# The expert stage of a PEER layer on one core: transposed weights from the host, sums kept in PSUM, unrolled rings

## What is computed

```
eidx, g = the 16 best experts of each head and their softmax   # P x 8 x 16
u   = expert_u[eidx]                       # (P, 8, 16, D)
act = gelu(einsum("phkd,pd->phk", u, x))
out = einsum("phk,phkd->pd", g * act, expert_v[eidx])
```

## Time and profile before

| | us |
|---|---|
| median of 3 runs | 4127.46 (4125.85 to 4132.15) |
| span of the profiled execution | 4126.5 |
| phases ahead of the expert stage | to about 1877 |
| expert stage | 1877 to 4051 |
| final phase | 4051 to 4126.5 |

### The profile page before, as it was taken

One profiled execution on the slowest core, in us unless ns is written; L12 is line 12 of the kernel. 1 busy time (PEld: TensorE's weight loads), 2 busy tenths in 40 slices (PEclk: granted clock), 3 DMA queues, 4 the chain that ended last, 5 costly groups with the idle time before them and its releaser, 6 DMA issues. The chain is left out here.

```text
span 4126.5 us, 52192 instructions
## 1 busy us (share of the span) xinstructions
PE 3607.3 (87%) x16733; PEld 2479.9 (60%) x16733; DVE 2800.2 (68%) x5843; ACT 798.0 (19%) x1845; POOL 1709.6 (41%) x1654
## 2 busy tenths in 40 slices
PE   8679899995857777846999999999999999999992
PEld 1435454442347777844667766777676776667771
DVE  1523233334938777898787877788777887778876
ACT  0101111012105787601111111111111111111110
POOL 0000000001105998705565655555555655555540
PEclk9689999997989999978999999999999999999996
DMA  7233433302241334407999999999989999999973
GB/s 253 80 57 37 36 47 51 34 6 103 82 144 43 90 86 103 115 2 260 351 328 337 349 322 348 328 351 327 337 322 351 333 336 343 327 354 326 350 271 112
DMA packets 453585, 870.03 MB, mean 211 GB/s; under 512 B 194637, under 2 KB 244045, under 8 KB 453206
## 3 DMA queue, kind: packets, MB, share of 16 engines
q0 software_dynamic: 153008, 555.83, 37.3%
q1 hardware_dynamic: 300344, 311.30, 26.0%
HBM read 805.98 MB, written 61.06 MB: 210 GB/s over the span
## 5 line engine op out<-in xcount | busy, mean ns | idle before, releaser
L1460 PE MATMUL v<-vb,w 128*128 128x512 f32 x2640 | 1159.2, 594 | 4.9 <-DVE acc L1547 4.9
L1444 POOL DMA_INDIRECT ring<-in_expert_u,eu x512 | 616.7, 1204 | 603.7 <-DVE dots L1532 300.2
L1460 PEld LDWEIGHTS v<-vb,w 128*128 128x128 f32 x2640 | 493.5, 191 | 577.9 <-issue 571.2
L1444 POOL DMA_INDIRECT ring<-in_expert_v,ev x512 | 612.0, 1195 | 441.0 <-DVE acc L1542 282.8
L1490 PE MATMUL a<-h2T_hi,uT 128*128 128x320 f32 x4096 | 713.8, 321 | 0.0
L1490 PEld LDWEIGHTS a<-h2T_hi,uT 128*128 128x128 f32 x4096 | 621.7, 188 | 61.2 <-issue 61.2
L1542 DVE SCALAR_TENSOR_TENSOR acc<-ring,wgt,acc 128x1024 f32 x508 | 650.7, 1281 | 10.3
L1532 DVE CUSTOM_DVE_ANT_1 ring<-ring,h2T 128x1024 f32<-128x1024 f32 x512 | 602.4, 1218 | 0.6 <-DMA ring<-in_expert_u,eu 0.6
L652 PE MATMUL z<-W,hT 128*128 128x512 f32 x1152 | 507.9, 594 | 23.3 <-DMA bh<-in_b_in 23.3
L1245 POOL TENSOR_SCALAR hotJ<-cst,pickT 128x128 f32<-128x128 f32 x560 | 424.9, 778 | 124.4 <-ACT pickT L1232 119.9
L1514 ACT ACTIVATE ga<-a 128x320 f32<-128x320 f32 x256 | 112.1, 438 | 1802.0 <-PE a L1490 1456.1
(11 more groups left out here) (266 smaller groups left out, 3216.0 us busy)
## 6 DMA issues: line engine op xcount, KB each, us to landing
ub<-in_expert_u SPq DMA_DIRECT2D x128, 512.0 KB
vb<-in_expert_v SPq DMA_DIRECT2D x32, 2048.0 KB
weight_d<-stage SPq DMA_DIRECT2D x10, 4096.0 KB, 20.9
wt<-weight_d SPq DMA_DIRECT2D x128, 320.0 KB, 5.3
wa<-in_w_ada SPq DMA_DIRECT2D x12, 2048.0 KB, 8.0
W<-in_w_in SPq DMA_DIRECT2D x32, 512.0 KB, 10.0
wq<-in_w_pq SPq DMA_DIRECT2D x4, 2048.0 KB, 17.0
ring<-in_expert_u,eu POOLq DMA_INDIRECT x512
```

The lines of the kernel that those rows point to most:

```text
L1444: pool.indirect_dma_start(ring[:, r, :], None, table, bass.IndirectOffsetOnAxis(idx[:, k % SLOTS:k % SLOTS + 1], 0)).then_inc(landed[r], 16)
L1460: mm = pe.matmul(vps[(NU * (s // GS) + u) % VB][:, :], w[:, gp, q, t * P:(t + 1) * P], vb[:, gp, q, h * 512:(h + 1) * 512], start=(q == 0) ...
```

## The change

- Layout: the host passes a second copy of `expert_u`, in which each block is already transposed (partition = place in D, then k, then expert). The eight transposes, the tile t and the first copy go. ScalarE copies the loaded block to `u_hi`, VectorE writes the low part over the raw block.
- Second product: still plain float32. The sums of token blocks 0 and 1 (KEPT = 2) stay in PSUM over all 128 blocks, four matmuls per block, one block behind the first product. The other three token blocks have six units per group, with two PSUM buffers in place of four. They are dealt by BEFORE, BETWEEN and AFTER. There is no group of zeros any more.
- The loop of four rounds is written out: 128 blocks in a row, `vb` a ring of seven blocks (512 KB each), `w` a ring of six. The weighting is one multiply of 640 columns, at the head of VectorE's next block; the subtraction stands behind six gathered rows. The gelu is written into `w` directly.
- The gathered sums go to `accg` and from there to `peer_d` in DRAM. The final phase loads them into z for blocks 5 to 8, and reads blocks 0 and 1 from PSUM.
- Semaphores of the phases ahead are cleared by POOL at the start of the routing phase and used again. SBUF is allocated from both sides. The phases ahead are otherwise as they were.

```diff
+NI = NK
+KEPT = 2
...
+            acc = keep("acc", [P, ND - KEPT, D])
+            kept = [late.enter_context(nc.psum_tensor(f"v_kept{t}", [P, D], F32)) for t in range(KEPT)]
...
+            for s in spent:
+                pool.sem_clear(s)
...
+    RV, RW = 7, 6
+    UNITS = [(t, h) for h in range(2) for t in range(KEPT, ND)]
...
+    BEFORE, BETWEEN, AFTER = {2: (4, 5)}, {1: (1, 2), 2: (5, 6)}, {0: (0, 1), 1: (2, 4)}
+    TAKE = {1: (0, 2), 2: (2, 5), 3: (5, 6)}
...
+            for n in range(NI):
+                if n >= 2:
+                    sp.wait_ge(act_ps, 2 * (n - 1))
+                sp.dma_start(u_raw[:, n % 2, :, :], a["expert_uT"][n]).then_inc(u_in[n % 2], 16)
+                if n >= RV:
+                    sp.wait_ge(unit_done, NU * ((n - RV) // GS + 1))
+                sp.dma_start(vb[:, n % RV, :], a["expert_v"][0, n * NK:(n + 1) * NK, :]).then_inc(v_in[n % RV], 16)
+                if n >= 2:
+                    sp.wait_ge(w_done, n - 1)
+                sp.dma_start(wt[:, n % 2, :], weight_d[n]).then_inc(wt_in[n % 2], 16)
+                g, s = divmod(n, RS)
+                if n == 0 or (s == RS // 2 + 1 and g + 1 < NG):
+                    at = 0 if n == 0 else g + 1
+                    if n:
+                        sp.wait_ge(used, 2 * SLOTS * g + SLOTS)
+                    sp.dma_start(h2, h2_d[TD + at * P:TD + (at + 1) * P, :].rearrange("t (k p) -> t k p", p=P)
+                                 ).then_inc(h2_in, 16)
+                if s == 2 and g > 0:
+                    sp.wait_ge(used, 2 * SLOTS * g)
+                    sp.dma_start(peer_d[(g - 1) * P:g * P, :], accg[:, :]).then_inc(gath_stored, 16)
+            sp.wait_ge(used, 2 * SLOTS * NG)
+            sp.dma_start(peer_d[(NG - 1) * P:NG * P, :], accg[:, :]).then_inc(gath_stored, 16)
+            sp.wait_ge(gath_stored, 16 * NG)
...
+                if k >= RING:
+                    pool.wait_ge(used, k - RING + 1)
...
+            def act_product(n, c):
+                cols = slice(c * HT, (c + 1) * HT)
+                if n >= 1:
+                    pe.wait_ge(gelu_done, 2 * (n - 1) + c + 1)
+                mm = chained(aps[c][:, :], [(u[:, n % 2, k, :], h[:, k, cols]) for u, h in
+                                            ((u_hi, hT_hi), (u_hi, hT_lo), (u_lo, hT_hi)) for k in range(KC)])
+                mm.then_inc(act_ps, 1)
+            def kept_product(n):
+                pe.wait_ge(v_in[n % RV], 16 * (n // RV + 1))
+                pe.wait_ge(w_done, n + 1)
+                for t in range(KEPT):
+                    cols = slice(t * P, (t + 1) * P)
+                    for h in range(2):
+                        half = slice(h * 512, (h + 1) * 512)
+                        mm = pe.matmul(kept[t][:, half], w[:, n % RW, cols], vb[:, n % RV, half],
+                                       start=(n == 0), stop=(n == NI - 1))
+                mm.then_inc(kept_done, 1)
+            def unit_product(grp, u):
+                t, h = UNITS[u]
+                cols, half = slice(t * P, (t + 1) * P), slice(h * 512, (h + 1) * 512)
+                at = NU * grp + u
+                if at >= 2:
+                    pe.wait_ge(unit_taken, at - 1)
+                mm = chained(vps[at % 2][:, :], [(w[:, n % RW, cols], vb[:, n % RV, half])
+                                                 for n in range(GS * grp, GS * grp + GS)])
+                mm.then_inc(unit_done, 1)
+            pe.wait_ge(hT_lo_done, 1)
+            for n in range(NI):
+                grp, s = n // GS - 1, n % GS
+                def units(where):
+                    for u in range(*where.get(s, (0, 0))) if grp >= 0 else ():
+                        unit_product(grp, u)
+                units(BEFORE)
+                pe.wait_ge(u_lo_done, n + 1)
+                act_product(n, 0)
+                units(BETWEEN)
+                act_product(n, 1)
+                if n >= 1:
+                    kept_product(n - 1)
+                units(AFTER)
+            kept_product(NI - 1)
+            for u in range(NU):
+                unit_product(NGRP - 1, u)
...
+            def split_u(n):
+                act.wait_ge(u_in[n % 2], 16 * (n // 2 + 1))
+                act.activation(u_hi[:, n % 2, :, :], u_raw[:, n % 2, :, :], ACT.Copy).then_inc(u_hi_done, 1)
+            act.activation(hT_hi[:, :, :], h2T[:, :, 0:TD], ACT.Copy).then_inc(hT_hi_done, 1)
+            split_u(0)
+            for n in range(NI):
+                if n % RS == RS // 2:
+                    act.wait_ge(used, 2 * SLOTS * (n // RS) + SLOTS)
+                    act.activation(wgt[:, :], dots[:, :], ACT.Gelu).then_inc(dots_gelu, 1)
+                if n + 1 < NI:
+                    split_u(n + 1)
+                if n >= RW:
+                    act.wait_ge(unit_done, NU * ((n - RW) // GS + 1))
+                for c in range(2):
+                    act.wait_ge(act_ps, 2 * n + c + 1)
+                    act.activation(w[:, n % RW, c * HT:(c + 1) * HT], aps[c][:, :], ACT.Gelu
+                                   ).then_inc(gelu_done, 1)
...
+            def weigh(n):
+                dve.wait_ge(wt_in[n % 2], 16 * (n // 2 + 1))
+                dve.wait_ge(gelu_done, 2 * n + 2)
+                v = w[:, n % RW, :]
+                dve.tensor_tensor(v, v, wt[:, n % 2, :], ALU.mult).then_inc(w_done, 1)
+            def split_u(n):
+                dve.wait_ge(u_hi_done, n + 1)
+                low(u_lo[:, n % 2, :, :], u_raw[:, n % 2, :, :], u_hi[:, n % 2, :, :]).then_inc(u_lo_done, 1)
...
+            dve.wait_ge(hT_hi_done, 1)
+            low(hT_lo[:, :, 0:TD], h2T[:, :, 0:TD], hT_hi[:, :, :]).then_inc(hT_lo_done, 1)
+            split_u(0)
+            for n in range(NI):
+                rows = iter(range(PER * n, PER * n + PER))
+                def gather(count):
+                    for k in itertools.islice(rows, count):
+                        gathered(k)
+                grp = n // GS - 1
+                takes = iter(range(*TAKE.get(n % GS, (0, 0))) if grp >= 0 else ())
+                def take_one():
+                    for u in itertools.islice(takes, 1):
+                        take(grp, u)
+                if n >= 1:
+                    weigh(n - 1)
+                take_one()
+                gather(2)
+                gather(1)
+                take_one()
+                gather(2)
+                take_one()
+                gather(1)
+                if n + 1 < NI:
+                    split_u(n + 1)
+                gather(2)
+            weigh(NI - 1)
...
+                if b >= ND:
+                    sp.wait_ge(y_stored[b % NZ], 16 * (b // NZ))
+                    sp.dma_start(z[:, b % NZ, :], peer_d[(b - ND) * P:(b - ND + 1) * P, :]).then_inc(peer_in[b % NZ], 16)
...
-                own.link(dve.tensor_tensor(v, acc[:, b, :], g2[:, b // NP, :], ALU.mult))
+                if b < KEPT:
+                    moe = kept[b][:, :]
+                elif b < ND:
+                    moe = acc[:, b - KEPT, :]
+                else:
+                    moe = v
+                    dve.wait_ge(peer_in[b % NZ], 16 * ((b - ND) // NZ + 1))
+                own.link(dve.tensor_tensor(v, moe, g2[:, b // NP, :], ALU.mult))
...
+    rows = np.asarray(inputs["expert_u"]).reshape(NI, NK, KC, P)
+    arrays["in_expert_uT"] = np.ascontiguousarray(rows.transpose(0, 3, 2, 1))
```

More of the change, by code:

```diff
@@ L136, in build @@
         h2_d = dram("h2_d", [NTOK, D])
[L138 to L150, removed]
+        peer_d = dram("peer_d", [NG * P, D])
         weight_d = dram("weight_d", [NK, NK, TD])
@@ new lines, in build, with front_sem, const @@
+            spent = []
+            def front_sem(name, software=False):
+                if software:
+                    return sem(name)
+                spent.append(front.enter_context(nc.semaphore(name)))
+                return spent[-1]
+            with ExitStack() as early:
+                cst = early.enter_context(nc.sbuf_tensor("cst", [P, NKEEP], F32))
+                ones = early.enter_context(nc.sbuf_tensor("ones", [P, P], F32))
+                def const(name, lo=0, n=None):
+                    at, w = CAT[name]
+                    return cst[:, at + lo:at + (w if n is None else lo + n)]
+                modulation_phase(nc, a, front_sem, mod_d, cst, ones, const)
+                with ExitStack() as mid:
+                    hB = mid.enter_context(nc.sbuf_tensor("hB", [P, NB, D], F32))
+                    gB = mid.enter_context(nc.sbuf_tensor("gB", [P, NB, D], F32))
+                    mixer_phase(nc, a, o, front_sem, mod_d, cst, ones, const, hB, gB)
+                    output_phase(nc, a, front_sem, mod_d, x1_d, h2_d, const, hB, gB)
+                with nc.sbuf_tensor("h2T", [P, KC, TD + P], F32, side="right") as h2T:
+                    routing_phase(nc, a, sem, h2_d, weight_d, const, h2T, experts, gates, spent)
@@ L168, in x_block @@
```

(25 more changed lines are left out.)

236 lines of the change are left out of this document (59 added, 177 removed).

## The result

| | us |
|---|---|
| median after, 4 runs | 3973.06 (3972.03 to 3976.02) |
| median before, same chip, 4 runs | 4126.66 |
| ratio, 95% interval | 0.9627 (0.9614 to 0.9641) |
| profiled execution after: span, its time | 3970.4, 3972.03 |
| forecast | 3977, range 3962 to 4060 |

The **opening** is the start of ScalarE's copy into `h2T_hi`, when the expert stage opens: 1877.33 before, 1866.83 after. The stage runs from there to the end of the last v row. A **hole** is idle time of TensorE ahead of a row; in the rows it is the figure in brackets, with what ended it.

What follows compares the result with a forecast made beforehand. TensorE's work was taken to bound the expert stage. Its terms (-14.4 -110.5 -24.0 -13.9 +2.8 +6.5) gave -153.6 us; with +3 for the final phase the span became 3975.9, forecast 3977, range 3962 to 4060.

Steps and rivals of the forecast that it cites:

- TensorE sets the end: Expert stage: TensorE's work sets its end, so a saved matmul is saved time until something else is late.
- Transposes, -110.5: Expert stage: 128 sets of transposes go, 127 of them behind the first a row, saving 110.5 us.
- Zeros, -24.0 and an earlier start: Expert stage start: group of zeros gone, 56 of its 80 rows behind 1902.96 save 24.0 us; first a row 14.4 earlier.
- Joints, -13.9: Expert stage: straight line instead of a loop of four removes the loop's joints, -13.9 us, bounds 9 and 14.
- First a row 1888.6: Expert stage start: first a row follows h2T's split and the first block's subtraction, at 1888.6, 14.4 us earlier.
- Cold clock +2.8 and stall +6.5: First blocks: TensorE coming from idle costs 2.8 us; waiting for transfers before the fifth block 6.5, bounds 0 and 20.
- Steady state: Four blocks cost 62.4 us; no listed wait of VectorE, ScalarE or SP reaches TensorE, smallest margin 2.6 us.
- Transfers 13.7 to 15.1 of 15.6 us: Expert stage: one block's 5.57 MB needs 13.7 to 15.1 us of transfers, under the 15.6 us pace.
- Final phase +3: Final phase: loads into z for blocks 5 to 8 come some 0.8 us late, four times: +3, bounds 0 and 10.
- Order of the phases ahead untouched, nothing for it: Phases before the expert stage: order unchanged, semaphore clears covered by POOL's wait in routing, so 0 us.
- The range: Whole kernel: the sum's own range from its terms' bounds was 3962 to 3998; the stated range was 3962 to 4060.

Runs made afterwards that it cites:

- host layout: Kernel before with only u transposed by the host and the eight transposes per block gone; 4016.74 us, ratio 0.9735.
- DRAM tensors: Kernel before with `expert_uT` and `peer_d` declared in DRAM and never used; 4125.24 us, ratio 1.0.
- the one with halves: Changed kernel with 4, then 9 and 10 gathered rows per block at the start, and the split of h2T in two halves; 3964.26 us, ratio 0.96.
- the extra load: Changed kernel with one more load of 512 KB per block, from expert_v into a tile nobody reads; 3975.73 us, ratio 0.9636.

## Why the prediction was right

- *TensorE sets the end*: right. Pitches unchanged, no hole in 1963 us behind the start; taking three quarters of the transfers away changed nothing there.
- *Transposes, -110.5*: -110.9 alone.
- *Zeros, -24.0 and an earlier start*: the gross figure stands, but it and the start-up stall are one thing. In the kernel before the zeros cover VectorE's and the gathers' start; taken away alone they bring 2.1 behind the first a row (2099.9 to 2097.8). The prediction booked a stall separately, so its sum held.
- *Joints, -13.9*: -13.0, and TensorE's program alone makes them.
- *First a row 1888.6*: 11.3 us after the opening, to the tenth; its clock time was 1878.1, since the stage opened earlier.
- *Cold clock +2.8 and stall +6.5*: **the mis-sized term**, 15.0 for 9.3: 10.5 of holes for 6.5, some 4.4 of slow stretches for 2.8. The prediction took the stall from bytes and bandwidth, with the fifth block as the one that waits. Two thirds of the 15.0 do go with the gathers' transfers. But each of the four blocks behind the first waits, since VectorE stands between transfers and TensorE with its rows ahead of each subtraction; and the hole of 3.74 us brought the granted clock down again for 3.4 us. With four rows per block no hole is left there, and 1.4 of the 15.0.
- *Steady state*: right where it matters. VectorE also waits for gathers, 67 us from 1935 to 3850, which the list didn't have, and none of it reaches TensorE. The smallest margin of the list, in the group shown: the subtraction for the next s0 ended at 2179.3, its block began at 2181.4, 2.1 us later (forecast 2.6). Landing of u 6.9 (6 to 8).
- *Transfers 13.7 to 15.1 of 15.6 us*: the share is 0.96, and with 9% more bytes the pace still holds.
- *Final phase +3*: -0.2. Of the four loads one made VectorE wait, 0.17 us. The failed step is an addition: the medians of 2.9 and 3.5 us run from the start of the issue, and the prediction added 0.53 for each issue on top. Without it 4085.03 + 2.9 + 3.5 is 4091.4, ahead of the 4091.56 at which it is wanted. VectorE's multiplies of two blocks after:

```profile
3935.09 1.22 DVE L1700 TENSOR_TENSOR f_z<-f_z,f_g 128x1024 f32<-128x1024 f32 x1
...
3942.25 1.23 DVE L1700 TENSOR_TENSOR f_z<-f_z,f_g 128x1024 f32<-128x1024 f32 x1 [0.17 <-DMA f_z<-peer_d]
```

- *Order of the phases ahead untouched, nothing for it*: wrong by 10.5 us. It and the 3.2 of the final phase offset the start's 5.7 and a stage otherwise 2.4 long. Most of the 2.4 is the changed kernel's own: four blocks take 62.53 us, in the two kernels that lack only the transposes or also the loop and the zeros 62.47, as the pitches add up. That the forecast is off by only 4 us is luck in part: misses of 14 and 8 us cancel.
- *The range*: "from the bounds above" does not give 3962 to 3998. Added up, the bounds of the start, the joints and the final phase reach from 3967 to 4002. The measured 3973 lies inside both, and inside the stated 3962 to 4060.

**Where the 10.5 us come from** is narrowed, not settled. They are in the mixer's first loop. Windows view of the kernel before, and of the one after, 400 to 450 us:

```profile
400.00:450.00 50.00, 33.08 (x109) 19.33 (x108) 11.47 (x39) 4.50 (x20) 2.91 (x4) 0.83 0.82 53
```

```profile
400.00:450.00 50.00, 43.65 (x142) 24.05 (x141) 14.21 (x49) 5.78 (x24) 2.90 (x4) 0.93 0.41 70
```

Twice the share for fewer bytes: the loads pass more slowly before, and TensorE waits for what hangs on them. Waits of TensorE (us in total, times, longest) and the loads of W (KB, us to landing) in the mixer, 250 to 600 and 250 to 590 us, before:

```profile
PE qk_ps L668 <- DVE zc L751: 19.5, 3, 13.5
```

```profile
W<-in_w_in SPq DMA_DIRECT2D x13, 512.0 KB, 12.2
```

and after:

```profile
PE qk_ps L683 <- DVE zc L766: 8.7, 3, 3.0
```

```profile
W<-in_w_in SPq DMA_DIRECT2D x15, 512.0 KB, 9.4
```

One wait of 13.5 us is what is gone, and a load of W takes 9.4 us in place of 12.2. The kernel in which only TensorE's loop was written out shows the same, with not a line of the mixer changed:

```profile
PE qk_ps L668 <- DVE zc L751: 8.1, 3, 3.0
```

```profile
W<-in_w_in SPq DMA_DIRECT2D x15, 512.0 KB, 9.5
```

In the fourteen profiles (before, after and twelve experiments) the stage opened at 1874.0 to 1877.3 in the three kernels whose TensorE loops in the expert stage (before, host layout, DRAM tensors) and at 1859.2 to 1867.5 in the eleven where that is written out, whatever else they do. Code that comes 1300 us later thus changes how loads run here. How is open: the length or place of TensorE's program in memory could do it, and no run tells these apart.

## What to carry to other kernels

When work is removed from the engine that sets the pace, look at what it was covering at the start of the stage. Here the first blocks, with half to two thirds of the work, were bound by the engine that feeds TensorE and by its transfers, and dealing that engine's side work unevenly (5, then 9, then 8 rows) was worth 12 us. The catch-up must be spread as well: ten rows per block were too many, nine were not (one hole of 0.30 us). Instructions removed from the engine that sets the pace count in full (110.9 for 110.5); of a whole kernel's time, expect some us from phases that the change doesn't touch.

## What the runs showed of the hardware

**A gather's issue waits for a long subtraction.** GpSimd's issue of one gather takes 0.94 us, but beside the subtraction of 5.49 us, which reads two tiles of SBUF, 6.16. In the changed kernel, and then in the one with halves:

```profile
1871.33 5.49 DVE L1550 TENSOR_TENSOR h2T_lo<-h2T,h2T_hi 128x5120 fp32r<-128x5120 f32 x1 [5.01 <-ACT h2T_hi L1532]
1871.47 6.16 POOL L1466 DMA_INDIRECT ring<-in_expert_u,experts  x1 [0.30 <-issue]
```

```profile
1869.84 2.82 DVE L1555 TENSOR_TENSOR h2T_lo<-h2T,h2T_hi 128x2560 fp32r<-128x2560 f32 x1 [2.87 <-ACT h2T_hi L1535]
1870.87 2.60 POOL L1466 DMA_INDIRECT ring<-in_expert_u,experts  x1 [0.30 <-issue]
```

Both issues end 0.81 us after the subtraction does; the one beside the second half's subtraction does too. Beside VectorE's adds of L1571, of which one input lies in PSUM, the issue stays at 0.94 (32 issues with no other work of VectorE beside them). That the second input from SBUF is the reason fits and isn't shown. The gather held back is the fourth, and VectorE waits 1.14 us for the fourth row at 1883.41: it had held that gather back itself.

**One core moved 392 GB/s for 1500 us**, with two thirds of the bytes in gathers, and 409 from 1880 to 1931, at the start of the stage, with the extra load.

**The same program's phases ahead differ by some us between executions** (3.7 here), so a profile of one execution places a stage's start no better than that; lengths inside the stage repeat to half a us.
